# A bias table built from 16 copies instead of 128, and an output projection fed two outputs at a time

## What is computed

```python
def gmlp_mixer(h, w_in, v_norm_g, w_s, b_s, w_out):
    z = jax.nn.gelu(h @ w_in)
    u, v = jnp.split(z, 2, axis=-1)
    v = rmsnorm(v, v_norm_g)
    ...
    s = jnp.einsum('gij,bnjgc->bnigc', w, v) + b_s.T[None, None, :, :, None]
    out = u * s.reshape(B, S, GMLP_WIDTH)
    return out @ w_out

def chunk_attention(h, k, v, w_q, rel_bias, w_o):
    ...
    rel_idx = jnp.clip(qi - kj + PAD, -REL_CLIP, REL_CLIP) + REL_CLIP
    bias = rel_bias[:, rel_idx].astype(jnp.float32)
    ...
        sc = jnp.einsum('bqhd,bkhd->bhqk', qb, kb).astype(jnp.float32) + bias
```

## Time and profile before

| | us |
|---|---|
| median of 3 runs | 2834.57 |
| lowest and highest | 2831.92, 2834.86 |
| the profiled execution, its own time | 2836.34 |
| its span in the trace | 2834.6 |
| TensorE busy in the span | 2641.1 (93%) |
| DVE, ACT, POOL busy | 839.5, 578.4, 441.6 |

### The profile page before, as it was taken

One profiled execution on the slowest core, in us unless ns is written; L12 is line 12 of the kernel. 1 busy time (PEld: TensorE's weight loads), 2 busy tenths in 40 slices (PEclk: granted clock), 3 DMA queues, 4 the chain that ended last, 5 costly groups with the idle time before them and its releaser, 6 DMA issues. The chain is left out here.

```text
span 2834.6 us, 27215 instructions
## 1 busy us (share of the span) xinstructions
PE 2641.1 (93%) x9849; PEld 1370.8 (48%) x9849; DVE 839.5 (30%) x1957; ACT 578.4 (20%) x1076; POOL 441.6 (16%) x397
## 2 busy tenths in 40 slices
PE   6999999999999999999999989999989999999992
PEld 5544444444566444444444447666745444344440
DVE  1023222102333232220022335556533322222215
ACT  2111111111333211110025533122111211111111
POOL 3004555500000100000121001101110111111110
PEclk9999999999999999999999999999988999999996
DMA  7315555432121122233232110000032799999985
GB/s 144 118 60 146 147 148 148 138 82 62 49 60 60 60 74 74 81 85 82 63 82 75 40 49 25 25 30 16 23 154 91 263 419 417 404 400 400 389 349 215
DMA packets 290831, 407.24 MB, mean 144 GB/s; under 512 B 14258, under 2 KB 253560, under 8 KB 264608
## 3 DMA queue, kind: packets, MB, share of 16 engines
q1 hardware_dynamic: 273504, 366.24, 37.3%
q0 software_dynamic: 16112, 37.19, 4.5%
q10 hardware_dynamic: 1104, 2.31, 0.2%
HBM read 396.20 MB, written 30.46 MB: 151 GB/s over the span
## 5 line engine op out<-in xcount | busy, mean ns | idle before, releaser
L906 PE MATMUL bank<-hT,bring 128*128 128x512 f32 x1344 | 582.1, 593 | 0.0
L906 PEld LDWEIGHTS bank<-hT,bring 128*128 128x128 f32 x1344 | 253.8, 190 | 311.9 <-issue 311.9
L845 PE MATMUL bank<-bring 128*128 128x512 f32 x704 | 303.3, 593 | 0.0
L1531 PE MATMUL bank<-bring 128*64 128x512 f32 (+1 forms) x512 | 227.0, 596 | 2.7 <-issue 1.7
L845 PEld LDWEIGHTS bank<-bring 128*128 128x128 f32 x704 | 133.5, 190 | 166.5 <-issue 166.5
L2023 DVE SCALAR_TENSOR_TENSOR ffw<-bank,col,ffw 128x511 f32<-128x511 f32 x88 | 66.0, 750 | 413.5 <-ACT ffw L1632 413.3
L1632 ACT ACTIVATE ffw<-bank,col 128x512 f32<-128x512 f32 x88 | 68.5, 778 | 492.7 <-PE bank L906 470.0
L2008 DVE TENSOR_TENSOR xT<-bank,xT 128x512 f32<-128x512 f32 x32 | 22.1, 691 | 377.3 <-PE bank L845 377.2
L1544 PE MATMUL bank<-bring,xT 128*64 128x512 f32 (+1 forms) x256 | 120.3, 614 | 9.1 <-DMA ysq<-exp_w_down 4.5
L1531 PEld LDWEIGHTS bank<-bring 128*64 128x64 f32 (+1 forms) x512 | 77.8, 157 | 97.4 <-issue 96.2
L1104 PE MATMUL bank<-hT,bring 128*128 128x512 f32 x256 | 118.5, 610 | 3.6 <-DVE ysq L2188 3.6
(11 more groups left out here) (475 smaller groups left out, 3604.2 us busy)
## 6 DMA issues: line engine op xcount, KB each, us to landing
bring<-f_w_in SPq DMA_DIRECT2D x88, 512.0 KB, 5.2
bring<-exp_w_gate SPq DMA_DIRECT2D x32, 1024.0 KB
bring<-exp_w_up SPq DMA_DIRECT2D x32, 1024.0 KB
bring<-exp_w_down SPq DMA_DIRECT2D x32, 1024.0 KB
two<-ada_w SPq DMA_DIRECT2D x24, 1024.0 KB, 5.4
bring<-f_w_down SPq DMA_DIRECT2D x16, 1408.0 KB, 6.9
two<-exp_w_gate SPq DMA_DIRECT2D x16, 1024.0 KB
two<-exp_w_up SPq DMA_DIRECT2D x16, 1024.0 KB
```

The costliest lines, as they stand in the source:

```text
L845: mm = pe.matmul(ps[BANKS[stage][n % 4]][:], w[:, k, n % per * P:(n % per + 1) * P], rhs[:, k, :], start=(k == 0), stop=(k == kb - 1))
L906: mm = pe.matmul(ps[2 * j + b][:], w[:, k, b * P:(b + 1) * P], hT[:, k, :], start=(k == 0), stop=(k == KB - 1))
L1531: mm = pe.matmul(ps[3][m * h:m * h + m, :].rearrange("p (m n) -> p m n", m=2), hgT[par][:, k, m * h:m * h + m], w, start=(k == 0), stop=(k ...
```

## The change

Two edits. The first makes the DRAM buffer smaller: 16 copies of each head's row instead of 128. Partitions are then loaded in eight groups of 16. For the group that begins at p, copy r of the 16 serves partition p + r, and the offset P - 1 - p at the start of the load gives the rest of the shift. The table that arrives is the same. The semaphore `rel_stored` now reaches 16 + 8 x 16 = 144, and DVE's wait for it is raised to that. The second edit lets TensorE run the k-outer part of the output projection over outputs 0 and 1 only; outputs 2 to 7 follow in `linear`.

```diff
-        rel_dram = scratch("rel_dram", 16, P, RELW + 1)
+        rel_dram = scratch("rel_dram", 16, 16, RELW + 1)
...
             pool.wait_ge(s("col_ready"), 2)
-            pool.dma_start(rel_dram[:, :, 0:RELW], relR[:].unsqueeze(1).to_broadcast([16, P, RELW]))\
+            pool.dma_start(rel_dram[:, :, 0:RELW], relR[:].unsqueeze(1).to_broadcast([16, 16, RELW]))\
                 .then_inc(s("rel_stored"), 16)
             pool.wait_ge(s("rel_stored"), 16)
-            pool.dma_start(biasT, bass.AP(rel_dram.tensor, 127, [[RELW, P], [P * (RELW + 1), 16], [1, 256]]))\
-                .then_inc(s("rel_stored"), 16)
-            pool.wait_ge(s("rel_stored"), 32)
+            for p in range(0, P, 16):
+                pool.dma_start(biasT[p:p + 16], bass.AP(rel_dram.tensor, P - 1 - p, [[RELW, 16], [16 * (RELW + 1), 16], [1, 256]]))\
+                    .then_inc(s("rel_stored"), 16)
+            pool.wait_ge(s("rel_stored"), 144)
...
             for k in range(KB):
-                for n in range(4):
+                for n in range(2):
                     pe.wait_ge(s("vn_ready"), TT + max(k, n) + 1)
                     linear_step("go", gT, KB, n, k)
-            linear("go", gT, KB, lambda k: None, done=[KB] * 4)
+            linear("go", gT, KB, lambda k: None, done=[KB] * 2)
             feed_forward(0)
...
             dve.wait_ge(s("consts"), NCONST)
-            dve.wait_ge(s("rel_stored"), 32)
+            dve.wait_ge(s("rel_stored"), 144)
```

## The result

| | before | changed |
|---|---|---|
| median, us (5 runs each on one chip) | 2834.57 | 2816.97 |
| lowest and highest | 2827.91, 2835.99 | 2813.20, 2821.47 |
| ratio with its 95% interval | | 0.9944 [0.9927, 0.996] |
| profiled execution, own time and span | 2836.34, 2834.6 | 2821.47, 2819.5 |

The changed kernel is 0.56% faster, 17.6 us by the medians, with an interval of 11 to 21 us; the two profiled executions differ by 14.9. The forecast was 2818.6, 16.0 us.

A forecast was written before the change was run, and what follows sets the result against it. TensorE, busy 93% of the span, was taken as the bound, with load waits of 16.6 and 3.6 us to cut. Gains of 9.4 + 6.6 = 16.0 us gave a median of 2818.6 us, range 2808.5 to 2825.

The forecast's parts named there:

- The store: POOL's store to rel_dram shrinks from 3.146 to 0.393 MB; 3.0 us fixed plus 4.0 of data, landing in 7.0 us.
- The loads' rate: POOL's eight 16-partition table loads run at the store's 98 GB/s, keeping q0 busy from 48.4 to 69.8 us.
- Which queue is ahead: Unit 3's load on q1 starts at 47.4 us, one microsecond before q0; 40 of 65 packets per engine through at 49.6.
- sign of being wrong: Forecast is wrong if 16 partitions don't slow a load, or q1's share beside q0 isn't one packet for one.
- The landing: Unit 3's load in the first projection has its data done at 66.4 us and lands 0.9 us later, at 67.3.
- The first term: TensorE's stall before unit 3 of the first projection falls from 16.6 to 7.1 us: 9.4 us gained.
- The second term: Output projection loses its 3.62 us wait for a_w_out and 2.96 us of slow clock: 6.6 us gained.
- The clock: A 7 us stall still costs TensorE's unit 3 2.0 us of slow clock; a stall under 3 us would save them.
- The side remark: With one output fed at a time, 0.86 us per block, TensorE would wait for DVE, which takes 1.51 us.
- Rival 1: No stall left before unit 3: 16-partition loads overlap, or its whole load goes ahead; 25.1 us gained, 2809.5; chance 0.33.
- Rival 3: Slower: the eight loads don't overlap, 5.7 us each, 46 us in all; stall 33 us, total 2844.5; chance 0.04.
- Rival 2: The second edit in the output projection doesn't do what it says; 9.4 us gained alone, 2825.2; chance 0.06.

The follow-up runs named there:

- split_only: Kernel before with the second edit and, of the first, only eight 16-partition loads (store still 128 copies): 2823.12 us, 0.997 of the kernel before.
- wide_spread: Both edits, table loaded by one 128-partition load with rows spread over 16 copies (wrong table): landed in 12.4 us, no wait before unit 3.
- one_wide: Both edits, table loaded by one 128-partition load from copy 0 (wrong table): load 26.2 us, wait 13.0 us, whole 11252 us with overflow rounds.
- table_only: First edit alone (16 copies, eight 16-partition loads), output projection still feeding four outputs: 2826.04 us, 0.9971 of the kernel before.
- loads_after: Both edits, POOL waiting for gv_prod 9 before issuing the eight loads: 2809.30 us, 0.9917 of the kernel before.
- pair_only: Second edit alone (two outputs fed together, table as before with 128 copies and one load): 2827.21 us, 0.9974 of the kernel before.

## Why the prediction was right, and where it was not

**The place and the mechanism** were right: POOL's slow store starved unit 3's load, and the order of the output projection made the slots come free too late. Each edit alone shows its own part.

**The store.** 4.0 us of data was right (q0 moves from 40 to 44 us), the fixed 3.0 us not; it landed in 5.6 us instead of 7.0. The fixed part had been taken as 35.1 less 32.1, where an error of some per cent in the rate is as large as the fixed part itself.

**The loads' rate.** I took the store's 98 GB/s. The burst moved 2.1 MB from 46 to 66 us, 105 GB/s beside q1, and alone it runs at 126. That the rate goes with the partitions agrees with split_only and wide_spread, but it is not all: a wide load out of one row goes at 127 GB/s too (one_wide, 48 to 52 us), and loads of 16 partitions differ by a third with the number of copies.

**Which queue is ahead** was wrong. The store landed 1.4 us sooner than I said, so POOL's loads were issued at 44.8 instead of 46.6, and their first packets came 1.2 us behind that instead of 1.8: q0 was first, at 46 instead of 48.4. The head start of q1 did not exist; its first packets came at 49 instead of 47.4. That should have cost 2 us or more. What followed had the right counts in the wrong place: 40 packets per engine before the one-for-one stretch (said: 40) and 24 within it (said: 25), but the first were through at 55 and not 49.6, and the second took 11 us and not 16.8. Two errors of over 5 us cancelled, and that the data was done at 66 where I said 66.4 is luck. The prediction had named it as a sign of being wrong if q1's share beside q0 is not one packet for one. From 49 to 55 us it was 649 to 89, and table_only shows the same from 50 to 56 us, 541 to 117. Why q1 got that much with all of the burst queued is not explained by what the prediction says on the order in the engines; that is open.

**The landing.** q1 has moved as many packets as the load has by 66, but unit 3 begins at 68.8: 2.8 us later, not 0.9. From 66 to 68.5 q1 moves 468 packets more, and by then 464 of its packets are of the next load, issued at 59.8. So some engines were already far into that one while others still had packets of unit 3's load.

**The first term** was thus 7.3 us (7.55 less 0.24 of slower products) instead of 9.4, inside its bounds of 4.2 and 18.5. **The second term** was 6.7 instead of 6.6. The clock did as said: it fell in the changed kernel's stall, and not in the kernels without one, where the 192 records of units 1 to 3 run in 41.6 us.

**The side remark** that one output at a time would wait for DVE was not worked out; it waits 0.2 us.

**The sum.** 16.0 said; 14.0 by the two terms in the profile, 14.9 between the profiled executions, 17.6 between the medians. The interval of 11 to 21 us holds them all; that the forecast of the median is off by only 1.6 us is in part the scatter of single executions, 8 us from the lowest to the highest. Rival 1, no stall, did not come true for the change, but loads_after shows how close it was: it needs the same loads issued 5.9 us later. Its first reading, that 16-partition loads would overlap and run like a wide one, is refuted by the 126 GB/s. Rival 3, the fixed 3.0 us paid by each load in turn, is refuted by the burst: eight loads in 20 us and not 46. Rival 2 by pair_only.

## What to carry to other kernels

A transfer that nobody waits for can still stop TensorE: before making it smaller, ask whether it can be issued when no urgent load is near. Here the order of issue was worth another 8 to 10 us on top of the change, for one wait on a semaphore. When a table is built from fewer copies, look at how many partitions each load still covers: the 2.7 MB less written paid for loads at a third of the rate. And when two slots feed four sums, finish two of them first.

## What was not expected of the hardware

A 128-partition load whose partitions all read the same 1.5 KB row of each head (their starts 4 bytes apart) ran at 127 to 129 GB/s while it was alone (48 to 52 us), at 92 beside q1 (54 to 66 us), and landed after 26.2 us (one_wide); it ran at 352 when the rows were spread over 16 copies (wide_spread, 49 to 50 us). Eight 16-partition loads in a row ran at 126 to 164 GB/s, more than the store from 16 partitions with its 98. And the wait before unit 3 differed between executions with the same burst, 9.0, 7.1 and 5.7 us, while waits behind the long store were 16.0 to 16.6.
